# Token-major key and query norms, a reordered delta-rule stage, and gate projections from split weights

## What is computed

```python
u, qkv, z, a_lg, b_lg, gate_a, gate_b = split(h @ w_in)
y_s5 = gelu(s5_ssm(u))                       # branch A
glu_a, glu_b = split(y_s5 @ w_s5_glu)
branch_a = glu_a * sigmoid(glu_b)
q, k, v = split(silu(causal_conv(qkv)))      # branch B: 4 heads of 128
q = q * rsqrt(sum(q * q) + eps)              # l2norm over a head's 128 channels
k = k * rsqrt(sum(k * k) + eps)
lower = strict(beta * (k @ k.T) * decay)     # per chunk of tokens and head
u_c, w_c = solve(lower + I, [v * beta, k * beta * exp(gc)])
o, S = chunk recurrence with attn = tril(q @ k.T * decay)
branch_b = (rmsnorm(o) * silu(z)) @ w_gdn_out
merged = sigmoid(gate_a) * branch_a + sigmoid(gate_b) * branch_b
out = merged @ w_out
```

## Time and profile before

| what | value |
|---|---|
| median of 3 runs | 2139.69 us (2136.61 to 2140.27) |
| the profiled execution | 2137.92 us, of it span of the trace 2136.1 us |
| mean granted TensorE clock | 0.958 |
| busy TensorE, VectorE, ScalarE, GpSimd | 2016.4, 1578.8, 1080.0, 133.9 us |
| second half of the mixer, layer 0 | 157.21 to 378.23 us (up to the start of wo) |
| the same, layer 1 | 801.09 to 1021.97 us |

### The profile page before, as it was taken

The page is one execution under the profiler, slowest core; times in us unless marked ns, Lnnn a source line. Parts: engine busy times, 40 slices in busy tenths (PEclk is TensorE's granted clock), DMA queues, the critical chain, the costliest instruction groups (busy, mean ns, idle before and its releaser), DMA issues.

```text
span 2136.1 us, 29895 instructions
## 1 busy us (share of the span) xinstructions
PE 2016.4 (94%) x11258; PEld 1675.9 (78%) x11258; DVE 1578.8 (74%) x2188; ACT 1080.0 (51%) x1308; POOL 133.9 (6%) x232
## 2 busy tenths in 40 slices
PE   7998999799998998899899999999999999999996
PEld 4776887699998876887778788787887877888784
DVE  6884526455565694626489998999989999899986
ACT  2124211245433114211268777777777777677773
POOL 3440000000002440000000000000000000000000
PEclk9999997999999999998989999999999999999998
DMA  8575233455553454224449999999989999999992
GB/s 334 192 265 187 83 122 135 153 193 183 177 167 100 143 178 166 102 104 147 143 156 373 360 348 321 341 366 348 366 326 336 369 345 354 322 353 371 338 345 99
DMA packets 142328, 523.88 MB, mean 245 GB/s; under 512 B 16112, under 2 KB 16624, under 8 KB 141424
## 3 DMA queue, kind: packets, MB, share of 16 engines
q1 hardware_dynamic: 140112, 508.82, 66.7%
q10 hardware_dynamic: 1440, 7.90, 0.9%
q0 software_dynamic: 640, 5.35, 0.7%
HBM read 515.57 MB, written 6.43 MB: 244 GB/s over the span
## 4 chain that ended last, share of the span: by engine, by line
PE 78%; DVE 14%; ACT 4%; issue 2%; POOL 2%; DMA 1%; ACTq 0%; DVEq 0%
PE bank L863 25%; PE bank L889 14%; PE bank L272 14%; PE bank L729 11%; PE bank L431 4%; DVE wlo L2018 3%; DVE arena L1322 2%; PE bank L810 1%; DVE arena L1612 1%; ACT whi L1165 1%; PE bank L850 1%; DVE slab L1556 1%; PE bank L703 1%; PE bank L716 1%; PE bank L447 1%
## 5 line engine op out<-in xcount | busy, mean ns | idle before, releaser
L2018 DVE TENSOR_TENSOR wlo<-ring,whi 128x1024 fp32r<-128x1024 f32 x756 | 910.4, 1222 | 164.3 <-ACT whi L1165 158.4
L1165 ACT ACTIVATE whi<-ring 128x1024 fp32r<-128x1024 f32 x756 | 799.4, 1059 | 315.5 <-PE bank L863 151.5
L272 PE MATMUL bank<-hT,ring 128*128 128x264 f32 x1408 | 335.4, 399 | 11.8 <-ACT hT L1013 5.1
L272 PEld LDWEIGHTS bank<-hT,ring 128*128 128x128 f32 x1408 | 275.1, 197 | 67.9 <-issue 15.2
L863 PE MATMUL bank<-whi,gh 128*128 128x512 f32 x896 | 285.8, 400 | 3.1 <-DVE wlo L2018 2.3
L863 PE MATMUL bank<-whi,gl 128*128 128x512 f32 x896 | 279.6, 393 | 0.0
L863 PE MATMUL bank<-wlo,gh 128*128 128x512 f32 x896 | 278.7, 392 | 0.0
L863 PEld LDWEIGHTS bank<-wlo,gh 128*128 128x128 f32 x896 | 168.2, 188 | 39.2
L863 PEld LDWEIGHTS bank<-whi,gl 128*128 128x128 f32 x896 | 168.0, 188 | 37.9
L863 PEld LDWEIGHTS bank<-whi,gh 128*128 128x128 f32 x896 | 161.1, 188 | 36.9 <-DVE wlo L2018 5.6
L889 PE MATMUL bank<-whi,eh 128*128 128x512 f32 x448 | 142.3, 399 | 3.2 <-DVE wlo L2018 3.2
(11 more groups left out here) (368 smaller groups left out, 2474.8 us busy)
## 6 DMA issues: line engine op xcount, KB each, us to landing
ring<-in_w SPq DMA_DIRECT2D x964, 512.0 KB, 5.2
arena<-in_gdn ACTq DMA_DIRECT2D x2, 2048.0 KB, 8.2
out_gdns<-arena POOLq DMA_DIRECT2D x2, 2048.0 KB, 8.1
xT<-in_x ACTq DMA_DIRECT2D x1, 1056.0 KB, 9.0
out_y<-hT SPq DMA_DIRECT2D x1, 1056.0 KB, 3.9
masks<-in_masks ACTq DMA_DIRECT2D x1, 512.0 KB, 11.1
cpk<-in_cpk SPq DMA_DIRECT2D x1, 512.0 KB, 6.7
bt<-in_bt SPq DMA_DIRECT2D x1, 512.0 KB, 7.0
```

The lines of the kernel that those rows point to most:

```text
L272: ins = pe.matmul(out, w, rhs, start=start, stop=stop)
L1165: act.activation(whi[:, m % SPL, :], ring[:, r, :], ACT.Copy).then_inc(sem("hi_done"), 1)
L2018: v.tensor_tensor(wlo[:, m % SPL, :], ring[:, (low.base + m) % RING, :], whi[:, m % SPL, :].bitcast(F32), ALU.subtract).then_inc(sem("lo_d ...
```

## The change

- The sums of squares of q and k come out token-major: for each head and group of tokens one matmul has the squares as stationary operand and a single column of ones as moving operand (24 matmuls into one bank, 24 columns). Root and inverse work on 128x24 values (`qn`). New batches `rk` and `rq` and the group `rs` spread the factors over the partitions, and VectorE multiplies k, then q, chunk by chunk; `kk` comes before `rq`, and `ktok` and `qk` behind.
- The inverse keeps only `pT`; `p` is one transpose of it at the end. The third square computes only `e`.
- ScalarE computes the gate's exponential, logarithm and sigmoid in the first half, and squares q and k before the GELUs. The samples' inputs are prepared right behind `rq`. ScalarE issues the write of the prompt's state.
- `UNITS` and `LATE` are given by names of steps. Units 3 to 23 use three fp32r matmuls for each block: ScalarE makes the high half of a weight slot two units ahead (`unit_high`), GpSimd the low half (`unit_low`), into three pairs of buffers. Activations are split likewise: `mh`, `uh` by ScalarE, `ml`, `ul` by GpSimd, `ml` only when units 0 to 2, which still read `hT`, are through.

```diff
 ADA_LATE = ((1, 0), (1, 2))
-UNITS = [4, 1, 4, 2, 2] + [0] * 7 + [1] * 3 + [0] * 4 + [1, 2, 2, 3]
-LATE = {0: 4, 2: 6, 4: 2, 20: 4}
-assert sum(UNITS) == 3 * KD and sum(LATE.values()) == ADA_S
+UNITS = {"y": 3, "norm": 1, "k": 1, "ln": 1, "e": 2, "sq0": 0, "pr0": 0, "sq1": 0, "pr1": 0, "sq2": 0, "pr2": 1, "turn": 1,
+         "yl0": 0, "x0": 1, "yl1": 1, "x1": 1, "yl2": 0, "x2": 1, "wt": 1, "vn0": 1, "vn1": 1, "skq": 2, "svt": 1,
+         "so": 1, "on": 3}
+LATE = {"y": 4, "k": 4, "ln": 2, "e": 2, "skq": 4}
+assert sum(UNITS.values()) == 3 * KD and sum(LATE.values()) == ADA_S
+WHOLE = UNITS["y"]
+SPLIT = sum(UNITS.values()) - WHOLE
...
+                def split_unit(u, names, xh, xl, kt):
+                    assert stream.pos == unit_at(l, u) and stream.blk == 0
+                    i = u - WHOLE
+                    hi, lo = usplit[i % 3]
+                    pe.wait_ge(sem("ulo_done"), SPLIT * l + i + 1)
+                    for half, name in enumerate(names):
+                        ps = open_bank(pe, name)
+                        for k in range(kt):
+                            b = slice((half * kt + k) * P, (half * kt + k + 1) * P)
+                            for n, (w, x) in enumerate(((hi, xh), (lo, xh), (hi, xl))):
+                                ins = pe.matmul(ps[:, 0:N], w[:, b], x[:, k, :], start=k == 0 and n == 0,
+                                                stop=k == kt - 1 and n == 2)
+                                if stream.owed:
+                                    ins.then_inc(used, 1)
+                                    stream.owed = False
+                        close(ins, name)
+                    stream.pos, stream.owed = stream.pos + 1, True
...
+                    if u < WHOLE:
                         project(("in", l, UT + S5_STEPS + u), lambda k: hT[:, k, :], KD)
+                    elif u < 2 * KD:
+                        if u == WHOLE:
+                            pe.wait_ge(sem("ml_done"), l + 1)
+                        split_unit(u, [("in", l, UT + S5_STEPS + u)], mh, ml, KD)
                     else:
                         m = u - 2 * KD
                         if m == 0:
-                            pe.wait_ge(sem("gelu_done"), UT * (l + 1))
-                        for half in range(2):
-                            project(("glu", l, 2 * m + half), lambda k: uT[:, k, :], UT)
+                            pe.wait_ge(sem("ul_done"), l + 1)
+                        split_unit(u, [("glu", l, 2 * m + half) for half in range(2)], uh, ul, UT)
                 def fill(step):
...
                 s5_y(l, UT - 1)
-                ada_slots(LATE[0])
-                pe.wait_ge(sem("qk_sq"), l + 1)
-                for i in range(2 * NH):
-                    ps = open_bank(pe, ("qkn", l, i))
-                    close(pe.matmul(ps[:, 0:N], ones[:, :], sq[:, i, :], start=True, stop=True), ("qkn", l, i))
-                fill(1)
+                ada_slots(LATE["y"])
...
+                pe.wait_ge(sem("qk_sq"), l + 1)
+                name = ("qkn", l)
+                ps = open_bank(pe, name)
+                for g in range(3):
+                    m = P if g < 2 else NB
+                    for i in range(2 * NH):
+                        a = 2 * NH * g + i
+                        ins = pe.matmul(ps[0:m, a:a + 1], sq[:, i, P * g:P * g + m], ones[:, 0:1], start=True, stop=True)
+                close(ins, name)
...
+                def spread(name, c, h0):
+                    at = 2 * NH * c + h0
+                    batch4((name, l, c), lambda o, h: pe.matmul(o, qn[:, at + h:at + h + 1].broadcast_to([P, P]), ident,
+                                                                start=True, stop=True))
+                pe.wait_ge(sem("qn_done"), l + 1)
+                for c in range(NC):
+                    spread("rk", c, NH)
+                fill("k")
+                for c in range(NC):
+                    taken(pe, ("rk", l, c))
+                    batch4(("kk", l, c), one(k(c), k(c)))
+                for c in range(NC):
+                    spread("rq", c, 0)
+                name = ("rs", l)
+                ps = open_bank(pe, name)
+                for i in range(2 * NH):
+                    a = 2 * NH * NC + i
+                    ins = pe.matmul(ps[:, NB * i:NB * i + NB], qn[0:NB, a:a + 1].broadcast_to([NB, P]), ident[0:NB, 0:NB],
+                                    start=True, stop=True)
+                close(ins, name)
                 for c in range(NC):
                     batch4(("ktok", l, c), lambda o, h: pe.transpose(o, k(c)(h), ident))
                 for c in range(NC):
-                    batch4(("kk", l, c), one(k(c), k(c)))
+                    taken(pe, ("rq", l, c))
                     batch4(("qk", l, c), one(k(c), q(c)))
-                fill(3)
+                fill("ln")
                 for c in range(NC):
                     pe.wait_ge(sem("ln_done"), NC * l + c + 1)
...
-                        batch4(("eT", l, s, c), one(at("e", c), at("eT", c)))
-                    fill(5 + 2 * s)
+                        if s < 2:
+                            batch4(("eT", l, s, c), one(at("e", c), at("eT", c)))
+                    fill(f"sq{s}")
...
-                        batch4(("p", l, s, c), one(at("eT", c), at("p", c)))
                         batch4(("pT", l, s, c), one(at("e", c), at("pT", c)))
-                    fill(6 + 2 * s)
+                    fill(f"pr{s}")
+                for c in range(NC):
+                    taken(pe, ("pT", l, 2, c))
+                    batch4(("p", l, c), lambda o, h: pe.transpose(o, mats["pT"][c][:, h, :], ident))
+                fill("turn")
...
+            def unit_high(l, u):
+                n = unit_at(l, u)
+                act.wait_ge(landed[n % RING], 16 * (n // RING + 1))
+                act.activation(usplit[(u - WHOLE) % 3][0][:, :], ring[:, n % RING, :], ACT.Copy).then_inc(sem("uhi_done"), 1)
...
+                if WHOLE <= u < WHOLE + SPLIT - 2:
+                    unit_high(l, u + 2)
...
+                    if m == UT + 3:
+                        act.wait_ge(sem("ax_done"), l + 1)
+                        then(act, act.activation(gd[:, 1, :], gd[:, 1, :], ACT.Exp, scale=-1.0), "a_gd")
+                        act.activation(gd[:, 3, 0:NH], col(l, "a_log"), ACT.Exp).then_inc(sem("a_ln"), 1)
+                        act.activation(gd[:, 1, :], gd[:, 1, :], ACT.Ln, bias=1.0).then_inc(sem("a_ln"), 1)
+                        act.activation(gd[:, 4, :], gd[:, 4, :], ACT.Sigmoid).then_inc(sem("a_ln"), 1)
...
+                act.wait_ge(sem("s_back"), JT // 2 * (l + 1))
+                act.activation(sq, cv[:, 0:2 * NH, :], ACT.Square).then_inc(sem("qk_sq"), 1)
+                act.activation(mh[:, :, :], hT[:, :, :], ACT.Copy).then_inc(sem("mh_done"), 1)
...
+                for u in (WHOLE, WHOLE + 1):
+                    unit_high(l, u)
                 act.wait_ge(sem("nrm_ss"), l + 1)
-                act.activation(nrm[:, :, :], nrm[:, :, :], ACT.Sqrt).then_inc(sem("nrm_root"), 1)
-                fill(2)
...
+                act.wait_ge(sem("sp_done"), l + 1)
+                act.dma_start(gdnp_out[l], s_pr).then_inc(sem("sp_out"), 16)
                 act.wait_ge(sem("sp_out"), 16 * (l + 1))
...
-            def qk_norms(l):
-                v.wait_ge(sem("s5_free"), l + 1)
-                for i in range(2 * NH):
-                    name = ("qkn", l, i)
-                    takes(v, v.tensor_scalar(nrm[:, i, :], filled(v, name)[:, 0:N], EPS, None, ALU.add), name)
-                v.tensor_copy(ini[:, 3:4], nrm[:, 0, 0:1]).then_inc(sem("nrm_ss"), 1)
+            def qk_sums(l):
+                if l == 0:
+                    d(v.memset(qn[:, :], 1.0))
+                name = ("qkn", l)
+                ps, n = filled(v, name), 2 * NH * NC
+                d(v.tensor_scalar(qn[:, 0:n], ps[:, 0:n], EPS, None, ALU.add))
+                takes(v, v.tensor_scalar(qn[0:NB, n:], ps[0:NB, n:n + 2 * NH], EPS, None, ALU.add), name)
+                v.tensor_copy(ini[:, 3:4], qn[:, 0:1]).then_inc(sem("nrm_ss"), 1)
+            def qk_roots(l):
                 v.wait_ge(sem("nrm_root"), l + 1)
-                d(v.reciprocal(nrm[:, :, :], nrm[:, :, :]))
-                q, k = cv[:, 0:NH, :], cv[:, NH:2 * NH, :]
-                v.wait_ge(sem("cv_silu"), 3 * (l + 1))
-                d(v.scalar_tensor_tensor(q, q, HD ** -0.5, nrm[:, 0:NH, :], ALU.mult, ALU.mult))
-                v.tensor_tensor(k, k, nrm[:, NH:2 * NH, :], ALU.mult).then_inc(sem("qk_done"), 1)
-                v.wait_ge(sem("qk_done"), l + 1)
+                d(v.reciprocal(qn[:, :], qn[:, :]))
+                q = qn[:, :].rearrange("p (g i) -> p g i", i=2 * NH)[:, :, 0:NH]
+                v.tensor_scalar(q, q, HD ** -0.5, None, ALU.mult).then_inc(sem("qn_done"), 1)
+            def scaled(l, name, c, h0):
+                ps = filled(v, (name, l, c))[:, :].rearrange("p (h t) -> p h t", h=NH)
```

(52 more changed lines are left out.)

150 lines of the change are left out of this document (71 added, 79 removed).

## The result

The change makes the kernel faster, by much less than I forecast: 2123.8 us (median of four runs) against 2140.0 us, a ratio of 0.9925 with a 95% interval of 0.9908 to 0.9943. The forecast was 2095 us with a range of 2072 to 2116, so the sign was right and the time lies outside the range. One of the four runs was disturbed (2816 us); it counts in that median alone, the ratio is without it, and the other three took 2121.4 to 2124.2 us, median 2123.5. The profiled execution took 2124.15 us, its span 2122.3.

What follows compares the result with a forecast made beforehand. TensorE's own work was taken to bound nine tenths of stage A, with stage B mixed; -21.9 (A), -1.0 (B) and +0.5 (first half) give -22.4 us a layer, -44.8 for both: 2095 us, range 2072 to 2116.

Steps and rivals of the forecast that it cites:

- Stage B: From the last state matmul's end to the start of projection `go`, 60.8 us before: forecast 1.0 us less a layer.
- `skq` cannot start before 12.3 us: Stage B: `skq` waits for the prompt's and then the samples' states to land; 14.0 before, gain 1.7 us.
- `so` needs VectorE's 4.41 us `vm`: Stage B: `vm` ends some 9.2 us behind `skq`, so `so` starts at about 32.6 us, before at 36.1.
- Units: Stage A: 14 filling units as three fp32r matmuls take 2.93 instead of 3.60 us each, 9.4 us less a layer.
- stage A: From the first filling unit to the last state matmul's end, 146.0 us before: forecast 21.9 us less a layer.
- GpSimd's holds: Stage A: low halves of 2.5 us hold VectorE between the norms and `e_done`; 2 us of wait taken, 0 to 5.
- The inverse: Stage A: eight batches go and eight one-record transposes come, 6.3 us less; 16 batches in 14.4 us without a gap.
- The spreads: Stage A: new batches `rk` and `rq` add 3.6 us and `rs` 1.1, together 4.7 us more a layer.
- The sums: Stage A: new narrow sums of squares take about what the old 4.1 us did; change zero.
- First half: Each layer's first half: gate table loads fall in ScalarE's idle time, five small VectorE instructions add 0.5 us (0 to 1).
- GpSimd holds more: Rival, chance 0.17: more low halves hold VectorE whole, 10.5 us a layer more than forecast, 2116 us.
- No change: Rival, chance 0.03: stage A is a chain of latencies and the records saved turn into gaps.

Runs made afterwards that it cites:

- e1: The changed kernel with the prompt's state moved, so the samples' states' load needs only the last reader of `pT` and starts about 10 us earlier: 2100.0 us, ratio 0.9814.
- e2: The changed kernel with the old order between `skq` and `so` (`svt` first, then the adaLN turn and both units), load unchanged: 2105.8 us, ratio 0.9847.
- e3: The changed kernel with both the early load of the samples' states and the old order between `skq` and `so`: 2086.8 us, ratio 0.9749.
- e6: The changed kernel with all 24 units in float32 as before, without high and low halves or activation splits: 2123.7 us, ratio 0.9931.
- e5: The changed kernel with all GpSimd low halves but a layer's first three only 128 of 1024 columns wide, the rest stale: 2111.5 us, ratio 0.9873.

## Why the prediction was wrong

The profiled execution was to be 2093.1 us and was 2124.15, 31 us more. By its own steps:

**Stage B, "-1.0 us (-4 to +3)": this is the step that failed.** It measured +10.0 and +9.5, that is 21.5 of the 31 us. Three of its sentences did not hold.

"`skq` cannot start before 12.3 us" named the right wait, and it started at 15.6 and 14.2. ScalarE's write of the prompt's state landed 5.3 and 5.4 us behind the state's end, not 3.9; and the load took 10.3 and 8.7 us, not 8.4 (ring loads ran beside it in both layers, so why one took longer is open). TensorE also came sooner than the "about 11" us, at 8.6. In the kernel before, the two units ahead of `skq` start 0.8 us behind a gap of 2.31 us and took 9.0 us from start to start:

```profile
306.33 9.05 PE L272 MATMUL bank<-uT,ring 128*128 128x264 f32 x32
```

In the change, without that gap, they took 6.0: 3.0 us less, where I had 1.3. So a wait of 7.0 us opened (5.6 in layer 1) where the prediction's own numbers gave 1.3.

"`skq` keeps its 11.1 us" was wrong behind that wait: 13.8 us.

"`so` needs VectorE's 4.41 us `vm`, which ends some 9.2 us behind `skq`": `so` started 12.6 us behind `skq`, because `svt` now stands behind a unit that runs slowly after `skq` (from 318.0 to 323.2 us). I saw the new wait in front of `so` and took it for the old start less a few us; I did not ask what the clock does behind a gap, though the earlier trace rows show exactly that for two other places. The part from `so` to `o_done` was 28.7 instead of 26, and `so` itself took 13.7 for 9.4. e1 and e2 show the two pieces, and e3 takes all of it back.

The other steps:

- **Units, "14 x 0.67 = 9.4 us less": the size for one unit was right, the net was not.** Split units ran 2.9 us apart. The sum has them at -9.4 with 5.8 us of waits for GpSimd and ScalarE against them, net -3.6; the change against e6 has 0.3 - 2.4 + 3.8 = 1.7 us in stage A of layer 0. In e5, where only the first three low halves are whole, the same stretches give 0.3 + 1.9 + 4.4 = 6.6. So the units did save TensorE's time, as "TensorE's own work for nine tenths" says, and the holds took most of it away.
- **GpSimd's holds, "From 0 to 5 us of wait; I take 2": too low.** From `lt` to `pT` they cost 4.3 and 3.0 us, and `rk`, behind the held copy, stands 0.9 and 0.8 us later than in e6: together 5.2 and 3.8 a layer, at the upper end of the bounds. The count of "0 to 3 us in hand" for VectorE was right (in e5 it is through with `e_done` 2.6 us before TensorE needs it), but the holds are longer than that. My reason for the low value, that only instructions with two SBUF inputs are held, does not stand (below). The low halves themselves last 2.37 us, as forecast.
- **Everything else of stage A was about right.** Without the units and GpSimd the terms were -6.3, +4.7, -13.65 and -3.0, together -18.25; e6 has -16.7 in layer 0 (129.3 us from 160.12). The inverse is 16 batches in 16.6 us, at a granted clock of 0.89 behind the gap, instead of 14.4. The spreads took 5.6 us for 4.7, as `rs` took 1.9 and not 1.1. The sums took 5.2 and 4.2 us for "zero" more than 4.0, and the gate batches behind them 3.8 for 2.0. From the sums to the first split unit it is 9.0 us in layer 0, just what the forecast has with 4.0 + 2.0 + 3.0 of wait, but by luck: there is no wait at that unit, TensorE comes to it at 182.5, when GpSimd has been through for under a microsecond. GpSimd's first low halves are waited for all the same, one step later, through VectorE's copy ahead of `rk`.
- **A reading of the rows.** The four gaps of the norms run from 1.06 to 3.88 us, not from 1.47; the 14.7 us are right.
- **First half, "+0.5": cannot be told.** It measured +2.5 and +0.7. But the last group of S5 outputs in the first half of layer 0 begins between 155.6 and 159.8 us in the nine kernels with the new first half, and between 155.4 and 158.2 in the three with the old one.
- **The rivals.** "GpSimd holds more" (0.17) gave 2116 and was the nearest, and is right for a part: with most of the low halves gone it is 12 us less, but still 2111.5. "No change: A is in truth a chain of latencies, and the records saved turn into gaps" (0.03) is right in that saved time turned into gaps, 1.36 and 2.15 us in stage A and 7.0 ahead of `skq`; but e6, without gaps up to `pT`, shows no chain of latencies in A. The loss of clock in stage B stood in no rival.

## What to carry over

When a stage in front of a transfer is made faster, compute when the transfer lands and what TensorE does until then; a wait that opens there is paid twice, since here the narrow work behind it ran at the lower clock. A faster filling unit is worth its saving only as long as no other engine's chain becomes the longer one. Follow what prepares the unit: here GpSimd's low halves made VectorE's chain to `e_done` 5.8 us longer, and that took back what the units had saved. Start a load by the last reader of its space, not by a write that only shares it.

## What the runs showed of the hardware

**GpSimd holds VectorE's copies too.** L1741 copies four columns within SBUF, one input, and takes 0.17 us when GpSimd rests. In layer 0 it begins at 183.01, in layer 1 at 819.25 us, while a low half is being made:

```profile
179.36 4.67 POOL L2264 TENSOR_TENSOR ulo<-ring,uhi 128x1024 fp32r<-128x1024 f32 x2
```

```profile
183.01 1.05 DVE L1741 COPY gd<-gd 128x4 f32<-128x4 f32 x1 [3.54 <-PE bank L453]
...
819.25 2.02 DVE L1741 COPY gd<-gd 128x4 f32<-128x4 f32 x1 [3.54 <-PE bank L453]
```

It ends at 184.06, GpSimd at 184.03. `rk` hangs on this copy, and so a copy of four columns moves all that follows; in e1 it took 2.97 us (layer 0), in e6, without low halves, 0.17. In the prediction I set this rule of the Trainium skill ("GPSIMD Engine Reference", section 1, Specifications) aside in favour of the rows of before. With "VectorE: DVE Perf Modes" (What auto-detection actually checks) it covers single-source operations between SBUF tensors, and the trace after agrees. VectorE's copies from PSUM (L1788, 0.69 us at 216.05, while a low half began) were not held.

**A gap and the clock behind it.** `skq`, 64 records of two columns: 13.81 us in all eight cases behind a gap of 5.3 to 7.4 us (the change, e2, e5, e6, both layers), 8.8 to 11.9 without one. `so`: 13.5 to 14.0 behind 2.95 us (the change, e1, e5), 11.0 to 12.6 behind 2.31, 8.7 to 11.4 without a gap. What decides within the last range is open: the clock falls during `skq` in each kernel (0.62 and 0.72 from 292 to 304 us in e1 and e3), and these runs don't tell when it comes back. In two other places the longer gap had the lower clock: over the 5 us from the first spread the granted clock is 1.00 behind 1.27 us (the change, layer 1) and 0.66 behind 2.28 us (e3, layer 1).

**Narrow sums.** The 48 records with one moving column took 5.2 and 4.2 us, with no gap ahead of them. The 16 gate records behind them took 3.8 us in both layers, 2.0 in the kernel before. The granted clock is 0.50 during them in layer 0 (178.7 to 182.5 us) and 1.00 from 184 us on. The clock of the sums and the gate batches, layer 0:

```profile
173.00:183.00 10.00, 10.00 (x76) 9.41 (x69) 1.34 (x10) 4.86 (x6) 8.78 (x4) 0.66 0.64 225
```
